# Expert retrieval on one Trainium2 core: one stage instead of two for the queries and the gathers, and the query products in plain fp32

## What is computed

```python
def peer(h, w_q, sub_keys, u_tab, v_tab):
    q = (h @ w_q).reshape(b, L, PEER_HEADS, 2, D_HALF)              # 8 heads, 2 halves of 128
    scores = jnp.einsum("blhtd,htkd->blhtk", q, sub_keys)           # 128 keys for each half
    sv, si = lax.top_k(scores, PEER_TOPK)                           # 16 best of each half
    ...                                                             # 16 x 16 sums of pairs
    top_s, pos = lax.top_k(cand_s, PEER_TOPK)                       # 16 best pairs: 16 experts
    idx = jnp.take_along_axis(cand_i, pos, axis=-1)
    gate = jax.nn.softmax(top_s, axis=-1)
    ...
        act = jax.nn.gelu(jnp.einsum("tkd,td->tk", u_tab[it], xt))  # dot with the gathered U row
        return jnp.einsum("tk,tkd->td", gt * act, v_tab[it])        # weighted sum of the V rows
```

## Time and profile before

| what | value |
|---|---|
| median of 3 runs | 5480.8 us (5477.13 to 5482.44) |
| the profiled execution | 5478.57 us, of which the span from the first instruction to the last is 5476.4 us |
| busy share of the span | PE 66%, DVE 62%, POOL 45%, ACT 27% |
| granted TensorE clock, mean | 0.808 of full speed |
| gathers | 1280, 1342 MB, 59.6% of the DMA engines' span |
| other plain transfers | 205 MB, 10.7% |

### The profile page before, as it was taken

One profiled execution on the slowest core, in us unless ns is written; L12 is line 12 of the kernel. 1 busy time (PEld: TensorE's weight loads), 2 busy tenths in 40 slices (PEclk: granted clock), 3 DMA queues, 4 the chain that ended last, 5 costly groups with the idle time before them and its releaser, 6 DMA issues. The chain is left out here.

```text
span 5476.4 us, 49922 instructions
## 1 busy us (share of the span) xinstructions
PE 3641.0 (66%) x16280; PEld 1992.6 (36%) x16280; DVE 3418.6 (62%) x6745; ACT 1484.7 (27%) x3656; POOL 2465.4 (45%) x1790
## 2 busy tenths in 40 slices
PE   9778988965555675555555556988986555555555
PEld 3577877841111341111111115777773111111111
DVE  1545657346777447776776766837345777777775
ACT  0244344222222222222222223325222222222221
POOL 0336333335555335555555553323334555555554
PEclk9888989987777787777777778988997777777777
DMA  8413102249999659999999993101227999999998
GB/s 311 167 61 133 70 24 73 81 185 414 414 405 417 254 214 411 415 406 415 409 410 407 410 414 138 64 31 53 79 85 287 419 406 408 415 406 420 410 412 370
DMA packets 232541, 1550.29 MB, mean 283 GB/s; under 512 B 40020, under 2 KB 41300, under 8 KB 46036
## 3 DMA queue, kind: packets, MB, share of 16 engines
q0 software_dynamic: 184320, 1342.26, 59.6%
q1 hardware_dynamic: 47962, 204.86, 10.7%
HBM read 1544.82 MB, written 2.20 MB: 282 GB/s over the span
## 5 line engine op out<-in xcount | busy, mean ns | idle before, releaser
L1594 PE MATMUL banks<-arena 128*64 128x512 f32 x5120 | 1744.8, 825 | 1508.6 <-ACT arena L1554 1505.1
L1473 POOL DMA_INDIRECT arena<-in_experts,arena x1280 | 1477.3, 1154 | 1578.4 <-PE banks L1594 1242.5
L1508 DVE CUSTOM_DVE_ANT_0 arena<-arena,token_copies 128x1024 f32<-128x1024 f32 x1280 | 1648.2, 1304 | 808.0 <-DMA arena<-in_experts,arena 758.0
L1594 PEld LDWEIGHTS banks<-arena 128*64 128x64 f32 x5120 | 415.8, 179 | 2718.0 <-ACT arena L1554 2071.8
L262 POOL TENSOR_TENSOR wide_low<-wide_blocks,wide_high 128x1024 fp32r<-128x1024 f32 x244 | 612.6, 2532 | 1132.8 <-ACT wide_high L252 1132.8
L1547 ACT ACTIVATE arena<-arena 128x2 f32<-128x2 f32 x640 | 131.2, 205 | 2176.9 <-DVE arena L1508 2171.2
L300 PE MATMUL banks<-activation_a,wide_high 128*128 128x512 f32 (+1 forms) x1568 | 583.7, 372 | 18.6 <-POOL wide_low L262 6.7
L302 PE MATMUL banks<-activation_a,wide_low 128*128 128x512 f32 (+1 forms) x1568 | 563.4, 359 | 0.0
L1554 ACT ACTIVATE arena<-arena 128x64 f32<-128x64 f32 x1280 | 376.3, 340 | 279.6 <-POOL arena L1310 239.6
L301 PE MATMUL banks<-activation_b,wide_high 128*128 128x512 f32 (+1 forms) x1056 | 384.7, 364 | 0.0
L300 PEld LDWEIGHTS banks<-activation_a,wide_high 128*128 128x128 f32 x1568 | 308.9, 197 | 68.6 <-POOL wide_low L262 8.1
(11 more groups left out here) (175 smaller groups left out, 4764.2 us busy)
## 6 DMA issues: line engine op xcount, KB each, us to landing
wide_blocks<-in_wide SPq DMA_DIRECT2D x170, 1024.0 KB, 4.8
arena<-in_experts,arena POOLq DMA_INDIRECT x1280
arena<-mod_rows SPq DMA_DIRECT2D x12, 512.0 KB
residual<-in_tokens SPq DMA_DIRECT2D x6, 512.0 KB
arena<-in_keys SPq DMA_DIRECT2D x3, 1024.0 KB
arena<-in_icnt_grid SPq DMA_DIRECT2D x2, 1024.0 KB
out_x<-residual SPq DMA_DIRECT2D x4, 512.0 KB
arena<-in_pool_w SPq DMA_DIRECT2D x3, 512.0 KB
```

The source lines that it names most:

```text
L1473: pool.indirect_dma_start(out=v.ring[:, g % RING], out_offset=None, in_=io["experts"], in_offset=bass.IndirectOffsetOnAxis(ap=c.idx[:, u % ...
L1508: last = nc.vector.tensor_tensor_reduce(out=u_row, in0=u_row, in1=k.copies[:, n % NJ], scale=1.0, scalar=0.0, op0=ALU.mult, op1=ALU.add, a ...
L1594: mm = nc.tensor.matmul(k.ps[j * QUAD:(j + 1) * QUAD, a + half], v.lhs[:, g % 4, j], v.ring[:, (g * NJ + j) % RING, D + half * BANK:D + (h ...
```

## The change

The two stages of a retrieval become one, `stage_peer`. On each engine there are two threads of work, `queries()` and `retrieve()`, written as generators that yield planned times in us from the stage's start; `weave` merges them at build time into one fixed order by planned time. Nothing is scheduled at run time.

- The queries are projected in plain fp32: 8 matmuls for each of the 16 projections, straight from the loaded weights. The splits on ScalarE, GpSimd and VectorE for them are gone, and the tokens are modulated once.
- Unit 0 is chosen as soon as projections 0 and 1 have their scores (planned time FIRST), and gathers may begin at FIRST + 14. FIRST is 34 for NT = 4 and 18 for NT = 2. The other projections, two K tiles at a time, stand between the V sums.
- Unit 1 is now matched, numbered and taken inside unit 0's gathers and dots (the condition `u >= 1` is gone).
- The token copies for the dots come from the transposed tokens: 8 matmuls of 128 moving columns for each half row in place of 2 of 512. For the first tile they use one PSUM bank in place of two.
- The keys lie where the norm rows will lie; so the norm rows and the gate row are loaded after the last scores.
- The merge stage no longer prepares two weight blocks for a following retrieval; the context's merge, which is followed by the latents' projection, still does, but both after the second tile's norm.

```diff
-            round_wides(k, act, w0 + n_wide)
+            round_wides(k, act, w0 + n_wide - 1)
             for t in range(NT):
                 norm_root(k, act, stats, t)
-                if t == 1:
+                if t == 1 and stream == CONTEXT:
                     round_wides(k, act, w0 + n_wide + 1)
 
...
-            cut_wides(k, pool, w0 + n_wide + 1)
+            cut_wides(k, pool, w0 + n_wide + (1 if stream == CONTEXT else -1))
...
-    ring, h2, scores, lhs, small, v.g2 = carve(k, RING * 2 * D, 4 * D, 4 * 2048, 8 * QUAD, 2592, D)
+    ring, h2T, scores, lhs, small, spare, modc = carve(k, RING * 2 * D, 4 * D, NT * 2048, 8 * QUAD, 2592, D, 16)
     v.ring = ring.rearrange("p (s c) -> p s c", s=RING)
-    v.raw_ring = ring
-    v.h2 = h2.rearrange("p (t c) -> p t c", t=4)
-    v.scores, v.lng, v.lnb = scores, k.rows[:, 0], k.rows[:, 1]
+    v.h2T = h2T.rearrange("p (t c) -> p t c", t=KT)
+    v.scores, v.g2, v.lng, v.lnb = scores, spare, k.rows[:, 0], k.rows[:, 1]
+    v.qT = spare.rearrange("p (a b) -> p a b", a=2)
+    v.keys = k.rows[:].rearrange("p a (m c) -> p (a m) c", c=P)
     v.lhs = lhs.rearrange("p (q j c) -> p q j c", q=4, j=NJ)
+    v.modc = modc.rearrange("p (a t) -> p a t", a=2)
...
-def stage_queries(k, layer, stream, w0):
...
+def weave(*threads):
+
+    heads = [[next(g, None), n, g] for n, g in enumerate(threads)]
+    while True:
+        live = [h for h in heads if h[0] is not None]
+        if not live:
+            return
+        first = min(live, key=lambda h: (h[0], h[1]))
+        first[0] = next(first[2], None)
+
+
+def stage_peer(k, layer, stream, w0, last_stage):
...
+    M = 2 * PEER_HEADS
+    N_BLOCKS = PEER_HEADS
...
+    PROJ, STEP = 2.0 * NT, 2.0 * NT
+    proj_at = lambda m: PROJ + STEP * m
+    FIRST = proj_at(3) + 2.0
+    ROW = 2.6
+    dot_at = lambda g: FIRST + 16.0 + ROW * g
+    copy_at = lambda n: FIRST + 13.0 + 3.0 * n if n < 2 * NJ else dot_at(n // (2 * NJ) * PEER_HEADS * TOPK - 1) + 5.0
+    freed_at = lambda q: dot_at(2 * q + 1) + 4.0
...
+        def _(sp):
+            sp.dma_start(v.modc, mods[3 * D:5 * D].rearrange("(a t p) -> p a t", a=2, p=P),
+                         allow_slow_non_contiguous=True).then_inc(k.cols_loaded.sem, 16)
+            sp.dma_start(v.keys, io["keys"][layer]).then_inc(k.loaded.sem, 16)
+            load_wides(k, sp, w0 + N_BLOCKS + WIDE_SLOTS)
+            sp.wait_ge(k.s_proj.sem, nth(k.s_proj, M))
+            for dst, src in ((v.g2, mods[5 * D:6 * D]), (v.lng, io["ln_g"][layer, 1]), (v.lnb, io["ln_b"][layer, 1])):
+                sp.dma_start(dst, src.unsqueeze(0).to_broadcast([P, D])).then_inc(k.loaded.sem, 16)
+            sp.wait_ge(k.loaded.sem, ld + 64)
...
+            def gather():
+                yield FIRST + 7.0
+                c.match(pool, 0)
+                yield FIRST + 14.0
+                c.masks(pool, 0)
+                for u in range(UNITS):
+                    for n in range(TOPK):
+                        g = u * TOPK + n
+                        yield freed_at((g - RING) // NJ) if g >= RING else FIRST + 14.0
+                        if n == 0:
+                            pool.wait_ge(k.idx_ready.sem, b0["idx_ready"] + u + 1)
+                        if g >= RING:
+                            pool.wait_ge(k.slot_free.sem, b0["slot_free"] + (g - RING) // NJ + 1)
+                        pool.indirect_dma_start(
+                            out=v.ring[:, g % RING], out_offset=None, in_=io["experts"],
+                            in_offset=bass.IndirectOffsetOnAxis(ap=c.idx[:, u % 4, n // NJ, n % NJ:n % NJ + 1], axis=0),
+                        ).then_inc(k.landed[g % RING].sem, 16)
+                        if n == 3 and u + 1 < UNITS:
+                            c.match(pool, u + 1)
+                        if n == RING - 1 and u >= 1:
+                            c.masks(pool, u)
+
+            weave(gather())
...
+                for m in range(M):
+                    yield proj_at(m + 2) + 1.0
+                    dve.wait_ge(k.s_proj.sem, nth(k.s_proj, m + 1))
+                    dst = v.scores.rearrange("p (t c) -> p t c", t=NT)[:, :, m * P:(m + 1) * P]
+                    nc.vector.tensor_copy(dst, k.ps[:, 5 + m % 2, 0:T].rearrange("p (t c) -> p t c", c=P)) \
+                        .then_inc(k.s_copied.sem, 1)
+
...
-                wsum = v.h2[:, t]
+                wsum = v.scores[:, t * 2048:t * 2048 + D]
...
+            def retrieve():
+                def best(u):
+                    dve.wait_ge(k.s_copied.sem, nth(k.s_copied, 2 * (u % PEER_HEADS) + 2))
+                    c.best_keys(dve, u)
+
+                yield FIRST
+                best(0)
+                c.best_pairs(dve, 0)
+                yield FIRST + 8.0
+                c.weigh(dve, 0)
+                c.number(dve, 0)
+                yield FIRST + 12.0
+                c.take_rows(dve, 0)
+                yield max(FIRST + 13.0, proj_at(5) + 2.0)
+                best(1)
+                c.best_pairs(dve, 1)
+                for u in range(UNITS):
...
+                        if n == 0 and u == 0:
+                            c.weigh(dve, 1)
+                        if n == 1 and u + 1 < UNITS:
+                            c.number(dve, u + 1)
+                        if n == 5 and u + 1 < UNITS:
+                            c.take_rows(dve, u + 1)
+                        if n == 6 and u + 2 < UNITS:
+                            best(u + 2)
+                        if n == 9 and u + 2 < UNITS:
+                            c.best_pairs(dve, u + 2)
+                        if n == 12 and u + 2 < UNITS:
+                            c.weigh(dve, u + 2)
...
+            weave(queries(), retrieve())
...
+                for kt in range(KT):
+                    yield PROJ / KT * (kt + 1)
+                    act.wait_ge(k.xt_ready.sem, nth(k.xt_ready, kt + 1))
+                    nc.scalar.activation(v.h2T[:, kt, 0:T], k.ps[:, 2 + kt % 2, 0:T], ACT.Identity,
+                                         bias=v.modc[:, 0, kt:kt + 1], scale=v.modc[:, 1, kt:kt + 1]) \
+                        .then_inc(k.h_ready.sem, 1)
+                for m in range(M):
+                    yield proj_at(m + 1) + 0.5
+                    act.wait_ge(k.q_proj.sem, nth(k.q_proj, m + 1))
+                    if m >= 2:
+                        act.wait_ge(k.s_proj.sem, nth(k.s_proj, m - 1))
+                    nc.scalar.copy(v.qT[:, m % 2, 0:T], k.ps[:, 2 + m % 2, 0:T]).then_inc(k.q_copied.sem, 1)
...
+            def retrieve():
+                yield FIRST + 6.0
+                c.softmax(act, 0)
+                yield FIRST + 12.5
+                c.take_gates(act, 0)
+                yield from copies(0)
+                yield max(FIRST + 13.0, proj_at(5) + 2.0) + 8.0
+                c.softmax(act, 1)
...
+                        yield dot_at(2 * g + 1) + 1.4
...
+                def score(m):
+                    pe.wait_ge(k.q_copied.sem, nth(k.q_copied, m + 1))
+                    if m >= 2:
+                        pe.wait_ge(k.s_copied.sem, nth(k.s_copied, m - 1))
+                    for t in range(NT):
+                        last = nc.tensor.matmul(k.ps[:, 5 + m % 2, t * P:(t + 1) * P],
+                                                v.qT[:, m % 2, t * P:(t + 1) * P], v.keys[:, m], start=True, stop=True)
+                    last.then_inc(k.s_proj.sem, 1)
+
+                yield 0.0
+                for kt in range(KT):
+                    if kt >= 2:
+                        pe.wait_ge(k.h_ready.sem, nth(k.h_ready, kt - 1))
+                    for t in range(NT):
+                        last = nc.tensor.transpose(k.ps[:, 2 + kt % 2, t * P:(t + 1) * P],
+                                                   k.res[:, tb + t, kt * P:(kt + 1) * P], k.ident[:])
+                    last.then_inc(k.xt_ready.sem, 1)
+                yield PROJ
+                pe.wait_ge(k.h_ready.sem, nth(k.h_ready, KT))
+                pe.wait_ge(k.loaded.sem, ld + 16)
+                for m in range(M):
+                    yield proj_at(m)
+                    n = w0 + m // 2
+                    if m % 2 == 0:
+                        pe.wait_ge(k.wide_landed[n % WIDE_SLOTS].sem, 16 * (n // WIDE_SLOTS + 1))
+                    if m >= 2:
+                        pe.wait_ge(k.q_copied.sem, nth(k.q_copied, m - 1))
+                    for kt in range(KT):
+                        if kt and kt % 2 == 0:
+                            yield proj_at(m) + STEP / KT * kt
+                        last = nc.tensor.matmul(k.ps[:, 2 + m % 2, 0:T],
+                                                k.wide[:, n % WIDE_SLOTS, kt, (m % 2) * P:(m % 2 + 1) * P],
+                                                v.h2T[:, kt, 0:T], start=(kt == 0), stop=(kt == KT - 1))
+                        if kt == 0:
+                            signal_used(k, last)
+                    last.then_inc(k.q_proj.sem, 1)
+                    if m % 2 == 1:
```

(30 more changed lines are left out.)

331 lines of the change are left out of this document (100 added, 231 removed).

## The result

The changed kernel takes 5358.53 us (median of 4 runs, 5353.59 to 5361.01) where the kernel before takes 5480.18: a ratio of 0.9777, 95% interval 0.976 to 0.9794, so 2.2% faster. The forecast was 5361. The profiled execution has a span of 5351.5 us, 124.9 less than before, and is the shortest of the four; the others have spans of 5356.6 to 5359.0.

What follows compares the result with a forecast made beforehand. Transfers of expert rows bound latent retrievals, TensorE the query stages. Gains 36 (context) + 43 + 43.5 (latents) - 3 (merges) = 119.5 us: span 5476.4 becomes 5357, median 5361. Forecast 5335 to 5400, chance 0.60; range 5305 to 5425.

Steps and rivals of the forecast that it cites:

- The overlap: Latent retrievals: remaining queries run beside gathers from 68 us after stage start, ending at 183 us; layer 1 gains 43.5 us.
- The term on which most hung: Latent retrievals from the first V sum: TensorE has 109 us of projections, scores, V sums, spreads and shape changes left.
- A: Rival, chance 0.15: TensorE doesn't bind and transfers never starve in the retrievals; 172 us gained, 5309 us.
- B: Rival, chance 0.17: fixed order stalls much more than 6 us, 25 more per latent stage, 10 in the context's; 5421 us.
- C: Rival, chance 0.06: TensorE stays at 1.2 GHz while queries run beside latent gathers, 109 us become 218; 5611 us.
- D: Rival, chance 0.02: the change doesn't do what it says, first gather stays behind the last projections; about 5478 us.
- The row loads: Three norm row loads per retrieval, 3.8 us, moved behind the last scores: forecast to cost nothing, their reader being far away.
- The next stage's weight blocks in layer 0: Layer 0's latent retrieval: two of three blocks now come beside gathers, 2 x 2.55 us off 48, leaving 43.
- the 1 us of collisions: Latents' merges: losing the weight block preparation was worth 1 us each by fewer collisions on the DVE.

## Why the prediction was right

**The mechanism and its main terms held.** The first gathers were forecast at S + 38.7 and S + 51.7 and came at S + 38.8, 49.8 and 50.4. The overlap was to end at S + 183; SyncE saw the last scores at S + 180.3 and 182.5, with TensorE busy throughout at a clock of 0.98. The term on which most hung, 109 us of TensorE work at 0.87 us a matmul and 0.1 us a change of shape, was read from two places of the trace before, and both prices held between V sums. (32 changes at 0.1 us are 3.2 us, not the 4 of the sum; the size of this slip is below everything else.)

**A was wrong for the reason given**: eight slots are cover that is spent once. The runs with spread or halved projections show what it needs, TensorE work at a density that the transfers can outlast, and even then the weight blocks and row loads keep their price. **B**: from the first V sum on TensorE waited less than 2 us in all in layer 1's overlap, where the forecast had 6; the order written out by hand stalls less than I allowed. **C**: the clock stayed at 0.98 over the overlap, in which projections stood in the gaps between V sums. The loop of the Trainium skill ("TensorE: Matmul & The Clock Gate", HAM oscillation), which this rival leaned on, did not set in here. No run tests that it was the projections that kept it away. **D** did not happen.

**Three terms were mis-sized, and over the whole kernel they nearly cancel.** The account goes by the 37th dot of a latent stage, whose row the forecast had at S + 183. In the changed kernel it is the one at 2016.95 in layer 0 and at 4125.01 in layer 1:

```profile
2015.80 1.21 DVE L1458 CUSTOM_DVE_ANT_0 arena<-arena,token_copies 128x1024 f32<-128x1024 f32 x1
...
2016.95 1.21 DVE L1458 CUSTOM_DVE_ANT_0 arena<-arena,token_copies 128x1024 f32<-128x1024 f32 x1
...
4123.87 1.22 DVE L1458 CUSTOM_DVE_ANT_0 arena<-arena,token_copies 128x1024 f32<-128x1024 f32 x1
...
4125.01 1.22 DVE L1458 CUSTOM_DVE_ANT_0 arena<-arena,token_copies 128x1024 f32<-128x1024 f32 x1
```

and in the kernel before these two:

```profile
2098.75 1.22 DVE L1508 CUSTOM_DVE_ANT_0 arena<-arena,token_copies 128x1024 f32<-128x1024 f32 x1
...
4248.96 1.23 DVE L1508 CUSTOM_DVE_ANT_0 arena<-arena,token_copies 128x1024 f32<-128x1024 f32 x1 [1.14 <-DMA arena<-in_experts,arena]
```

That is S + 182.7 and S + 184.8 after, S + 230.4 and S + 225.6 before. So 47.7 and 40.8 us had been gained by then (forecast 48 and 43.5), and at the last dot 46.8 and 42.2.

1. The row loads. "The norm rows wait on SyncE for the last scores ... so it costs nothing" looked at who waits for them, not at what they displace. I also took 3.8 us off the way from the first gather to the first row because they had gone, without adding their bytes where they went. They cost about 3.5 us in each stage. In the context stage this is most of the miss: 36 - 3.5 = 32.5 for a measured 31.5. Its first V sum was 4 us late as well, which looked like the cause, and is not.
2. The next stage's weight blocks in layer 0. I took 5 us off for two of them landing beside gathers. They were issued at S + 136.4 and S + 158.1, where TensorE sets the pace, and there a second load of a block cost next to nothing (0.3 us by the run with doubled weights).
3. The dots' lag. Behind the 37th dot the forecast took 5 us off in layer 0 and nothing in layer 1; measured are 0.9 off and 1.4 added, though the row loads come there. What gives their time back seems to be that rows have landed ahead: two dots in a row start 1.15 us apart here, and the 37th starts 14.4 us behind its gather's issue, against 11.5 and 10.0 us in the kernel before. So there are 2.9 and 4.4 us to catch up, which the forecast did not have. As an estimate, with the 3.5 of the row loads, that gives 47.7 + 2.9 - 3.5 = 47.1 and 40.8 + 4.4 - 3.5 = 41.7, measured 46.8 and 42.2. The pace alone scatters by 1.5 us a stage, so this account is no finer than that, and no run tests it.

The 4 us of the context's merge and the 4 of the latents' (forecast 5 and 2) are small terms that I did not test; no row shows the 1 us of collisions that the forecast named for the latter.

**Where the early start went.** Of the 36 us that each latent stage loses against gathers with nothing beside them, TensorE's surplus is 16 and 19 (by the wider spread) and the row loads 3.5. With the queries spread, a second load of the blocks costs 15.2 and 6.4 us up to gather 192, so the first load should cost about as much; no run takes it away. In layer 0 this nearly closes the account (15.2 + 3.5 = 18.7 of the 19.8 left), in layer 1 some 6 of 16.3 us stay open. In the context 3.5 and 10.1 of 17.8 are accounted for; the other 4 are not settled. The start of the transfers is thin there (289 GB/s over the 10 us from the first gather), but the run with the gathers last starts thinly as well (310 GB/s), so this is worth some 0.5 us of it at most.

## What to carry to other kernels

When a stage that computes is laid over a stage that transfers, ask of each stretch which of the two sets its pace: a transfer moved into a stretch bounded by TensorE was nearly free here (0.3 to 0.6 us for 1 MB, within the scatter), and the same transfer in a stretch bounded by the DMA engines cost 2.0 to 2.4. "Nobody waits for it" prices only the latency of a load, not its bytes. A ring of eight buffers hides a late consumer once but not a surplus of work that lasts, so spread that work over as much of the transfer as the data's first use allows; and put nothing ahead of the first transfer to repair a wait that the ring already covers.

## What the runs showed of the hardware

- Where the DMA share was 1, plain loads from SyncE among gathers from GpSimd cost most of their own transfer time: 10.2 us of row loads added 9.1 to 9.7 us, and a 1 MB weight block, 2.55 us, added 2.0 to 2.4. In the changed kernel such a block took 4.8 us to land with little beside it, up to 8.8 us beside gathers in the latent stages and up to 10.5 in the context's.
- Plain fp32 products and V sums of another shape ran in turn for 110 us at a granted clock of 0.98. In three 50 us stretches with TensorE busy for 46.0, 39.4 and 38.0 us the clock was 1.00, 0.87 and 0.90. Behind the overlap it was 0.76, with TensorE busy 54%.
- The pace of the steady retrieval, from gather 64 or 192 on, is the same in all kernels here, 2.533 to 2.556 us a gather of 1 MB, and its scatter, not an edit, is the limit of what a single stage can tell.
